# A hybrid mixer layer: the Mamba step sizes and the DeltaNet gates computed in GLA's low-rank block, the Mamba gate stage folded into its projection, DeltaNet's output gate and block gathers moved

## The reference, cut to what matters

```python
u_l = modulate(x, norm_g[i, 0], sh1, sc1) @ w_in[i]          # columns: GLA 800, Hyena 768, Mamba 1032, DeltaNet 1040
# GLA: 32 low-rank columns (768:800) feed the decay gates
z = jnp.einsum('blsr,srk->blsk', lr, w2) + b
# Mamba, on tokens of the latent grid in column-major order; dt_raw = its last 8 columns
dt = softplus(dt_raw.reshape(b_, l_, N_DIR, MB_HEADS) + dt_bias)
a = -exp(a_log)                                              # cumulative sums of dt * a give the decays
# DeltaNet; beta_raw and a_raw = its last 16 columns, og = 256 columns before them
beta = sigmoid(beta_raw)
g = -exp(a_log) * softplus(a_raw + dt_bias)
m = where(strict, (k_beta @ k.T) * decay, 0)                 # per chunk and head, then the solve with (I + m)
sol = triangular_solve(m + I, rhs)
out = head_rmsnorm(o, norm_w) * silu(og)
```

## Time and profile before

| | |
|---|---|
| median of 3 runs (lowest, highest) | 2170.61 (2168.0, 2174.12) |
| the profiled execution's own time | 2176.57 |
| its span, first to last instruction | 2174.5 |
| PE, DVE, ACT, POOL busy | 1782.7, 1175.5, 837.2, 321.5 |
| mean granted TensorE clock | 0.896 |

### The profile page before, as it was taken

The page is one execution under the profiler, slowest core; times in us unless marked ns, Lnnn a source line. Parts: engine busy times, 40 slices in busy tenths (PEclk is TensorE's granted clock), DMA queues, the critical chain, the costliest instruction groups (busy, mean ns, idle before and its releaser), DMA issues. The chain is left out here.

```text
span 2174.5 us, 20430 instructions
## 1 busy us (share of the span) xinstructions
PE 1782.7 (82%) x7774; PEld 1221.8 (56%) x7774; DVE 1175.5 (54%) x1356; ACT 837.2 (39%) x1101; POOL 321.5 (15%) x402
## 2 busy tenths in 40 slices
PE   6897889965896838497989889991399999999981
PEld 3344654465454727493434773550288888888861
DVE  3612922168224265364432341337798888888873
ACT  4112222321224426263200000342277777777762
POOL 0000300021000324710040430320011010101000
PEclk9998989978898959798969899995699999999996
DMA  8712000020000442231041213213399999999964
GB/s 348 249 69 79 1 1 0 0 79 1 0 0 0 148 138 85 71 86 67 0 140 39 78 71 134 72 54 126 131 384 395 387 385 402 381 402 386 400 240 174
DMA packets 102569, 337.20 MB, mean 155 GB/s; under 512 B 32170, under 2 KB 41949, under 8 KB 77769
## 3 DMA queue, kind: packets, MB, share of 16 engines
q1 hardware_dynamic: 96048, 317.16, 38.6%
q0 software_dynamic: 4608, 16.78, 3.1%
q10 hardware_dynamic: 1817, 1.97, 0.3%
HBM read 303.83 MB, written 32.04 MB: 154 GB/s over the span
## 5 line engine op out<-in xcount | busy, mean ns | idle before, releaser
L2702 DVE TENSOR_TENSOR w_lo<-w_raw,w_hi 128x2048 fp32r<-128x2048 f32 x192 | 438.5, 2292 | 65.3 <-ACT w_hi L2648 65.2
L2648 ACT ACTIVATE w_hi<-w_raw 128x2048 fp32r<-128x2048 f32 x192 | 367.8, 1917 | 137.4 <-PE ps L2606 134.1
L482 PE MATMUL ps<-hT,w_mixer 128*128 128x512 f32 (+1 forms) x864 | 344.9, 560 | 4.4 <-PEq L186 2.5
L482 PEld LDWEIGHTS ps<-hT,w_mixer 128*128 128x128 f32 x864 | 165.3, 193 | 173.9 <-issue 169.1
L2604 PE MATMUL ps<-w_hi,xsT_hi 128*128 128x512 f32 x512 | 202.8, 396 | 2.4 <-DVE xsT_lo L2707 2.4
L2606 PE MATMUL ps<-w_hi,xsT_lo 128*128 128x512 f32 x512 | 200.4, 391 | 0.0
L2605 PE MATMUL ps<-w_lo,xsT_hi 128*128 128x512 f32 x512 | 200.2, 391 | 0.0
L2431 PE MATMUL ps<-w_out,yT 128*128 128x512 f32 x256 | 114.3, 602 | 3.4 <-DMA router<-in_moe_router 3.4
L2604 PEld LDWEIGHTS ps<-w_hi,xsT_hi 128*128 128x128 f32 x512 | 96.8, 189 | 22.0 <-DVE xsT_lo L2707 2.8
L2606 PEld LDWEIGHTS ps<-w_hi,xsT_lo 128*128 128x128 f32 x512 | 96.5, 189 | 20.3
L2605 PEld LDWEIGHTS ps<-w_lo,xsT_hi 128*128 128x128 f32 x512 | 96.7, 189 | 19.3
(11 more groups left out here) (443 smaller groups left out, 2880.7 us busy)
## 6 DMA issues: line engine op xcount, KB each, us to landing
w_raw<-in_moe_w_gate SPq DMA_DIRECT2D x64, 1024.0 KB, 7.0
w_raw<-in_moe_w_up SPq DMA_DIRECT2D x64, 1024.0 KB, 8.8
w_raw<-in_moe_w_down SPq DMA_DIRECT2D x64, 1024.0 KB, 8.7
w_mod_row<-in_w_mod SPq DMA_DIRECT2D x32, 512.0 KB, 5.0
w_mod<-in_w_mod SPq DMA_DIRECT2D x8, 1024.0 KB, 14.5
dn_ma<-dn_ma SPq DMA_DIRECT2D x16, 512.0 KB, 3.3
dn_rel<-dn_cum SPq DMA_DIRECT2D x20, 256.0 KB, 4.4
dn_mT<-dn_ma SPq DMA_DIRECT2D x20, 256.0 KB, 3.6
```

The source lines that it names most:

```text
L482: last = nc.tensor.matmul(S.ps[:, 3 * (i % 2) + c, 0:n], S.w[:, k, b["col"]:b["col"] + P], S.hT[:, k, t0:t0 + n], start=(k == 0), stop=(k ...
L2648: nc.scalar.activation(wh[q % RING][:, :], S.raw[q % RAW][:, :], ACT.Copy).then_inc(s.hi, 1)
L2702: nc.vector.tensor_tensor(wl[q % RING][:, :], S.raw[q % RAW][:, :], wh[q % RING][:, :].bitcast(F32), ALU.subtract).then_inc(s.lo, 1)
```

## The change

1. Two small loads behind GLA's weights bring Mamba's 8 step-size columns and DeltaNet's 16 gate columns beside the 32 low-rank columns; the gaps are set to zero. The low-rank block becomes 128 columns wide; ten small transposes and two ACT copies bring the new rows to tokens (`S.dt`, `S.dn_raw`, kept from there on).
2. The last block of `mb_c` and that of `dn_c` are gone, and `mb_t` with them; its work is a side computation (`MambaGates`) of `mb_c`.
3. In `dn_a` the output gate of tile 0 stands ahead of the units and those of tiles 1 to 7 after the matmuls of unit 12. All gathers go to one tile (`dn_block_u`) from which two copies take them (`take_blocks`, signal `taken`). Units 8 to 13 are gathered in `dn_a`, 14 and 15 at the start of `dn_s`, 16 to 19 ahead of step 3's loads; the loads of `dn_mT` stand ahead of the first write of inverses.
4. Buffers move by some hundred bytes: the new tiles (960 bytes a partition) stand ahead of `yT`, the experts' buffers start 960 bytes lower and the raw weight buffers lie 960 bytes higher.

```diff
-WCOLS = 1040
+WCOLS = 1024
...
+            for at, col, n in ((GLA_COLS + 32, MB0 + MB_COLS - 8, 8), (GLA_COLS + 64, DN0 + DN_COLS - 16, 16)):
+                src = A["w_in"][0, :, col:col + n].rearrange("(p k) n -> p k n", p=P)
+                sp.dma_start(S.w[:, :, at:at + n], src).then_inc(S.w_ready, 16)
+                S.w_count += 16
...
+            for a, b in ((0, 32), (40, 64), (80, 96)):
+                nc.vector.memset(S.w[:, :, GLA_COLS + a:GLA_COLS + b], 0.0)
...
-        lr = plan.take("gla_lrT", [33, TOK])
+                            "summed k_turned kt_out g_turned g_out rows_done rows_st") as s:
+        lr = plan.take("gla_lrT", [P, TOK])
...
-        cms = ((0, P, qT, GLA_DK ** -0.5), (P, P, kT, 1.0), (768, 32, lr, 1.0))
+        cms = ((0, P, qT, GLA_DK ** -0.5), (P, P, kT, 1.0), (768, P, lr, 1.0))
...
+            ident = S.t("ident")[64:P, 64:P]
+            pe.wait_ge(s.kt_out, 3)
+            for t in range(T):
+                last = nc.tensor.transpose(S.ps[:, 6 + t // 5, t % 5 * 64:t % 5 * 64 + 64], lr[64:P, t * P:(t + 1) * P], ident)
+            last.then_inc(s.g_turned, 1)
...
+                    if dst is lr:
+                        src, d = S.ps[64:96, q % 6, 0:n], lr[64:96, t0:t0 + n]
+                        if t0 >= CTX:
+                            r0 = (t0 - CTX) // GRID_W
+                            src = src.rearrange("p (r w) -> p r w", w=GRID_W)
+                            d = lr[64:96, CTX:TOK].rearrange("p (w r) -> p r w", r=GRID_H)[:, r0:r0 + 8, :]
+                        nc.scalar.activation(d, src, ACT.Copy)
+                        nc.scalar.activation(lr[96:P, t0:t0 + n], S.ps[96:P, q % 6, 0:n], ACT.Copy)
+                        m = 32
...
+            act.wait_ge(s.g_turned, 1)
+            rows = S.ps[:, 6:8, 0:320].rearrange("p b (t c) -> p b t c", c=64)
+            nc.scalar.activation(S.dn_raw[:, :, :].rearrange("p (b t) c -> p b t c", b=2), rows[:, :, :, 32:48], ACT.Copy)
+            dtf = S.dt[:, :, :, :].rearrange("p (b t) d h -> p b t (d h)", b=2)
+            nc.scalar.activation(dtf, rows[:, :, :, 0:8], ACT.Copy).then_inc(s.g_out, 1)
...
+    def pe(self, s, pe, i):
+
+        if i == 4:
+            pe.wait_ge(s.sp, 1)
+            gate_sums(self.nc, self.S, s, pe, self.ga, 0).then_inc(s.sums, 1)
...
+    def act(self, s, act, i):
+        nc, ab = self.nc, self.abs
+        if i == 0:
+            act.wait_ge(s.biased, 1)
+            nc.scalar.activation(ab[:, :], self.flat(self.dt), ACT.Abs).then_inc(s.ab, 1)
+            act.wait_ge(s.ab, 1)
+            nc.scalar.activation(ab[:, :], ab[:, :], ACT.Exp, scale=-1.0).then_inc(s.e1, 1)
+            act.wait_ge(s.e1, 1)
+            nc.scalar.activation(ab[:, :], ab[:, :], ACT.Ln, bias=self.S.one[:, 0:1]).then_inc(s.e2, 1)
+            nc.scalar.activation(self.rate[:, :], self.S.gates[:, 0, :], ACT.Exp).then_inc(s.ea, 1)
+        if i == 5:
+            act.wait_ge(s.sums, 1)
+            nc.scalar.activation(self.eu[:, :, :, :], self.sums(), ACT.Exp).then_inc(s.ea, 1)
...
+    def dve(self, s, dve, ch, i):
+        nc, rate = self.nc, self.rate
+        if i == 0:
+            dtf = self.by_token(self.dt)
+            nc.vector.tensor_tensor(dtf, dtf, self.S.gates[:, 1, :].unsqueeze(1).to_broadcast([P, T, 8]), ALU.add
+                                    ).then_inc(s.biased, 1)
+        if i == 1:
+            dve.wait_ge(s.e2, 1)
+            ch(nc.vector.scalar_tensor_tensor(self.flat(self.dt), self.flat(self.dt), 0.0, self.abs[:, :], ALU.max, ALU.add))
+            dve.wait_ge(s.ea, 1)
+            ch(nc.vector.tensor_scalar(rate[:, :], rate[:, :], -1.0, None, ALU.mult))
+            nc.vector.tensor_tensor(self.by_token(self.ga), self.by_token(self.dt),
+                                    rate[:, :].unsqueeze(1).to_broadcast([P, T, 8]), ALU.mult).then_inc(s.sp, 1)
+        if i == 5:
+            dve.wait_ge(s.ea, 2)
+            ch(nc.vector.tensor_copy(self.cu[:, :, :, :], self.sums()))
...
-    blocks.append(dict(col=MB_COLS - P, tap=66, step=1, bias=None, silu=False, colmajor=True, cm=None,
-                       tok=dt[:, :, :, :].rearrange("p t d h -> p t (d h)"), sub=P - 8))
-    project_conv(nc, S, A, "mb_c", blocks, Plan(nc, small))
-    with Stage(nc, "mb_t", "biased ab e1 e2 ea sp chain sums") as s:
...
+    project_conv(nc, S, A, "mb_c", blocks, Plan(nc, small), side=gates)
...
-    raw = Plan(nc, SBUF_END - 4 * T * 16).take("dn_raw", [P, T, 16])
-    blocks.append(dict(col=DN_COLS - P, tap=66, step=1, bias=None, silu=False, colmajor=False, cm=None, tok=raw,
-                       sub=P - 16))
     project_conv(nc, S, A, "dn_c", blocks, Plan(nc, work_at))
-    gates_and_norms(nc, S, A, qt, kt, qT, kT, raw, ga, be, bec, cu, eu, dec, Plan(nc, mark))
+    gates_and_norms(nc, S, A, qt, kt, qT, kT, S.dn_raw, ga, be, bec, cu, eu, dec, Plan(nc, mark))
...
-        dst = (bu, bl)[d]
...
-    def turn_upper(ops):
-
+    def take_blocks(ops):
+
+        ops.tensor_copy(bl[64:P, :, :], bu[64:P, :, :])
         return ops.tensor_copy(bl[0:64, :, :], bu[0:64, :, :].rearrange("q r c -> q c r"))
...
+            sp.wait_ge(s.taken, 1)
+            for n in range(DN_GROUP, HEAD):
+                collect(n)
+            sp.wait_ge(s.zeroed, 1)
+            for st in range(2):
+                load_mt(sp, st)
             sp.wait_ge(s.sub, 1)
             put_blocks(sp, 0, s.d_st)
             for n in range(HEAD, N):
@@ -1391,12 +1435,10 @@
                 m = n - HEAD
                 if m == 0:
                     sp.wait_ge(s.d_st, 16)
-                if m == 1:
-                    sp.wait_ge(s.zeroed, 1)
-                if 1 <= m <= 4:
-                    load_blocks(sp, (m - 1) // 2, (m - 1) % 2)
-                elif m in (5, 6):
-                    load_mt(sp, m - 5)
+                if m in (0, 1, 4, 5):
+                    load_blocks(sp, m // 4, m % 4)
+                elif m in (2, 3, 6):
+                    collect(HEAD + (m - 2 if m < 4 else 2))
...
+            def gate(t):
+                if t >= 1:
+                    pe.wait_ge(s.og_out, t)
+                for k in range(KD):
+                    last = nc.tensor.matmul(S.ps[:, 7, 0:DG], S.hT[:, k, (CT + t) * P:(CT + t + 1) * P],
+                                            S.w[:, k, 768:768 + DG], start=(k == 0), stop=(k == KD - 1))
+                last.then_inc(s.og, 1)
+
             pe.wait_ge(S.w_ready, S.w_count)
+            gate(0)
...
+                if n == HEAD + 1:
+                    for g in range(1, LT):
+                        gate(g)
...
-                if n < LT:
-                    if n >= 1:
-                        pe.wait_ge(s.og_out, n)
-                    for k in range(KD):
-                        last = nc.tensor.matmul(S.ps[:, 7, 0:DG], S.hT[:, k, (CT + n) * P:(CT + n + 1) * P],
-                                                S.w[:, k, 768:768 + DG], start=(k == 0), stop=(k == KD - 1))
-                    last.then_inc(s.og, 1)
...
-                if 1 <= n <= LT:
-                    act.wait_ge(s.og, n)
-                    nc.scalar.activation(og[:, n - 1, :], S.ps[:, 7, 0:DG], ACT.Copy).then_inc(s.og_out, 1)
+                for g in range(LT):
+                    if n == (0 if g == 0 else HEAD + 2):
+                        act.wait_ge(s.og, g + 1)
+                        nc.scalar.activation(og[:, g, :], S.ps[:, 7, 0:DG], ACT.Copy).then_inc(s.og_out, 1)
...
-                if n == LT + 1:
+                if n == HEAD + 2:
...
-            ch(turn_upper(nc.vector))
+            take_blocks(nc.vector).then_inc(s.taken, 1)
+            dve.wait_ge(s.taken, 1)
...
-            for n in range(DN_GROUP, 2 * DN_GROUP):
+            for n in range(HEAD + 3, 2 * DN_GROUP):
                 gather(sp, n)
-                if n == DN_GROUP + 3:
-                    sp.wait_ge(s.z, 2)
-                    for d in range(2):
-                        load_blocks(sp, 2, d)
-                    load_mt(sp, 2)
-                    load_attn(sp, 2)
-            for st in range(3, T):
+            for st in range(2, T):
+                if st == 3:
+                    sp.wait_ge(s.taken, 1)
+                    for n in range(2 * DN_GROUP, N):
+                        gather(sp, n)
                 if st in (4, 8):
                     g = st // 4
                     sp.wait_ge(s.sub, g)
                     put_blocks(sp, g, s.d_st)
                     sp.wait_ge(s.d_st, 16 * g)
-                    if g == 1:
-                        for n in range(2 * DN_GROUP, N):
-                            gather(sp, n)
                 sp.wait_ge(s.z, 2 * st - 2)
...
-                pc(turn_upper(nc.gpsimd))
+                take_blocks(nc.gpsimd).then_inc(s.taken, 1)
+                pool.wait_ge(s.taken, g)
...
-    S.moe_at = S.hT_at - KD * SEQ * 4
+    S.moe_at = gates_at
...
-    S.raw_at = S.x1_at - 12288 - EARLY * 8192 - 3520
+    S.raw_at = S.x1_at - 12288 - EARLY * 8192 - 2560```

```

(1 more changed line is left out.)

66 lines of the change are left out of this document (24 added, 42 removed).

## The result

The changed kernel took 2111.54 us (median of 4 runs, 2109.10 to 2114.05) against 2170.43 for the kernel before on the same chip: a ratio of 0.973, 95% interval 0.971 to 0.975, or 2112.2 on the 2170.61 shown above. In a second set of runs the ratio was 0.972 (0.970 to 0.974), 2109.0. Forecast were 2097 and a range that ended at 2112: the sign came out, but 12 to 15 of the 74 us did not come. A profile of each kernel (the first of before, with a span of 2174.5, and the one of after, 2107.0) gives the ledger by stages.

The account below looks back on a forecast made before the run. Four limits by stage: TensorE in the projections, an idle, half-clocked PE beside DVE's substitution in dn_a, POOL's late substitution in dn_s. 3.8 - 26.8 - 18.2 - 10 - 22.8 = -74.0 from 2170.61, predicted 2097, range 2086 to 2112.

Parts of the forecast that it names:

- dn_a: DeltaNet stage dn_a: gates moved out of the units, write of the inverses earlier; saves 10, bounds 0 to 15.
- GLA: GLA's stage: ACT's copy in three pieces, PE's wait and ten transposes cost 3.8, between 2.5 and 5.5.
- Mamba: Mamba's projection: block 8 and its tail go, twelve small matmuls come; saves 26.8, between 25 and 28.
- dn_c: DeltaNet's projection: one block less, last copies to tokens 0.4 longer; saves 18.2, between 17.5 and 18.8.
- SP's queue is the next late thing, at 2.88 a unit: In dn_a's units without gates: 2.88 in place of 5.31 a unit, 17.0 over seven intervals of gathers.
- The start is even: Start of dn_a: tile 0's gate at the slow clock delays unit 0, units 0 to 2 lose theirs; no net change.
- I add 1: dn_a after the write of the inverses: nine stores, three more gathers, four loads fewer; 1 more than the earlier 22.9.
- dn_s: Stage dn_s: inverses 16.4 earlier, four gathers (6.4) out of the way; step 4's wait shrinks 22.8, bounds 19 to 24.
- The gates didn't stay at 1.2 GHz: Rival in dn_a: gates run at 1.2 GHz after sparse products, dn_a loses 16, total 2123; chance 0.05.
- POOL's substitution beside DVE's scan: Rival: POOL and DVE hinder each other, substitution stretches by a quarter, wait shrinks only 13.5, total 2106; chance 0.07.
- The second wait went: Rival in dn_s: step 4 keeps its wait because another link is last, 22.8 left out, total 2119; chance 0.04.
- ACT and DVE in the experts: Rival: experts' buffers moved by 960 bytes slow each of 192 weight pieces; 0.45 a piece gives 2183; chance 0.02.

Follow-up runs that it names:

- the twelve: Profiles of the changed kernel, its repeat and the follow-up edits of it, all with the new projections; one profile a kernel.
- after_again: Changed kernel run once more without an edit, for a second profile: 2107.69, ratio 0.972 to the kernel before.
- second pair: Second profiles of both kernels, run again without an edit: before 2170.59 (ratio 0.999), changed 2107.69 (ratio 0.972).

## Why the prediction's time was too low

The forecast was wrong by 12 to 15 us. The step that failed is the term for `dn_a`, 10, of which 0.8 to 3.1 came: its mechanism, SP's queue as the next bound, was right, and the price of SP's issues was not. The terms one by one:

- **GLA** (3.8): the three copies, the wait for the k copies and the transposes came as worked out, 3.9 to the token products in the first pair. The way from `gla_p`'s first matmul to `mb_c`'s grew from 216.7 and 219.9 in the two profiles of before to 222.3 to 224.4 in the twelve with this part: 3.8 in the first pair and 6.1 in the second. No wait at `w_ready` showed: PE's 7.96 ahead of the stage is the same as before. The first is as foretold, the second just outside the bounds (2.5 to 5.5).
- **Mamba** (26.8): from `mb_c`'s first matmul to the first product of `mb_s` on POOL 170.1 became 141.8, and 140.1 in seven of the twelve: 28.2 or more, over the bound of 28. The 1.8 between these two kinds isn't the change's: in after_again the granted clock is 1.00 from `mb_c`'s first matmul on, in after it is 0.50 for the first 3 us. `gate_sums` inside the dense block took 1.3 where I had 1.9, and a tail of 1024 columns ended sooner than mine.
- **`dn_c`** (18.2): 128.8 became 110.3, 18.5. `dn_l` behind it, which keeps its instructions, grew by 2.0 to 2.2. Of these 0.46 is the longer last copy to tokens (0.69, where 0.23 stood), which the 18.2 holds as its 0.4; so the term was right. The other 1.6 (below) the sum didn't hold.
- **`dn_a`** (10) is the step that failed. "SP's queue is the next late thing, at 2.88 a unit": it was the next late thing, at 3.84. The seven intervals from the first gather to the eighth took 27.1 (678.37 to 705.45) in place of 35.6 (725.90 to 761.52): 8.5 less, where I had 17.0. "The start is even": the first gather came 4.3 earlier, which hid half of that miss. So the copy came 12.5 earlier instead of 17 (9.7 against the second profile). "The write ... 11 earlier": 8.7 and 7.0. "I add 1": 5.6 and 6.2, for three gathers in a queue that is the bound of that stretch, for a wait that now came with one store ahead of it where before it had two, and for the inverses landing 5.8 to 6.3 after their issue, with the four loads of `dn_mT` right ahead of them, where before it was 2.7 (rows below). Left over of the 10: 3.1 in the first pair of profiles, 0.8 in the second.
- **`dn_s`** (22.8): the wait of 31.4 became 8.04 (foretold 8.6), the path to step 4 23.7 shorter, and the stage up to the head norm 22.6 (24.0 in the second pair). POOL's copy came 8.2 after the stage's start (9 to 10). Right.
- **Hyena's start** lost about 2 in most profiles (below), which I had at nothing. Not all of it reached the end: from the head norm to the transposes ahead of the experts 363.0 became 364.5 in the first pair, 364.7 and 364.6 stand in the second.

SP's queue in the kernel before, from the write of the inverses to the first loads that wait for it, with two stores in between:

```profile
791.86 0.32 SPq L1302 DMA_DIRECT2D dn_d<-dn_block_inv  x1
793.11 0.32 SPq L1371 DMA_DIRECT2D dn_ma<-dn_ma  x1
...
795.21 0.32 SPq L1371 DMA_DIRECT2D dn_ma<-dn_ma  x1
...
796.05 2.42 SPq L1311 DMA_DIRECT2D dn_diag<-dn_d  x4
```

Summed over the first pair, with 1.4 for everything behind the head norm: 3.8 - 28.2 - 18.5 + 2.0 - 3.1 - 22.6 + 1.4 = -65.2, and 2.3 more by which `gla_p` happened to start earlier: the 67.5 between the spans. The medians are 59 to 62 apart, 6 to 8 less: the profile of before was of an execution 6.0 above its median, which I allowed for, and that of after of one 2.4 below its own. In the second pair `dn_a`'s 0.8 for 10 is the largest miss, then GLA (2.3) and `dn_l`, with Mamba (3.4) and `dn_s` (1.2) the other way.

**The rivals.** The gates didn't stay at 1.2 GHz: the granted clock is 0.50 in the first us and 1.00 from the third on (0.97 from 706 to 738), the first gate took 4.43 and the rest 3.72. POOL's substitution beside DVE's scan took 37.1 (780.16 to 817.29) as before; DVE's took 24.3 against 24.5, with one operation of 1.15 beside a product on POOL, as the 1.30 before. The second wait went. ACT and DVE in the experts kept their times (L2747 2.29 a piece). All four are out. The range ended at 2112 because I let one term at a time reach its bound; `dn_a` near its own, with 2 to 3 for `dn_l` and Hyena that had no term at all and the scatter of the executions, used it up.
